# The opening of a one-core layer kernel by quarters of the channels, and a new order of its gates

## The chip, the core and the metric

One core of a Trainium2 chip. The metric is the device time of one execution in microseconds; the kernel before takes 708.6 us (median of three runs, 707.45 to 708.78). All data are f32. Products of activations with the big weights are split: a tile is cut into a high part (rounded to fp32r) and a low remainder, and a product is high x high + high x low + low x high, three fp32r matmuls.

## What is computed

One layer of a hybrid encoder, 256 tokens of 1024 channels, cut from the reference to what the change touches:

```python
c_act = jax.nn.silu(c)
mod = c_act @ ada_w[l] + ada_b[l]
sh1, sc1, gt1, sh2, sc2, gt2 = [m[:, None, :] for m in jnp.split(mod, N_MOD, axis=-1)]
h = rms_norm(x, norm1_g[l]) * (1.0 + sc1) + sh1
proj = h @ w_in[l]
q, k, v, g_out, gk_low, z, xbc, dt_raw, gates = split_cols(proj, IN_SIZES)
o_a = gla_mixer(q, k, v, g_out, gk_low, ...)
o_b = ssd_mixer(z, xbc, dt_raw, ...)
```

After it come the merge of both branches, a mixture of 32 experts (96 MB of weights) and the last norm. In the GLA mixer k is scaled by exp of sums of gates (gk), each chunk of 64 tokens gives an update k^T v, and the states follow by a recurrence over four chunks. In the SSD mixer a matrix exp(-|sum of rates|) per head is multiplied by C B^T of the chunk.

## The kernel before

**Pieces and units.** The weights come from HBM in pieces of 1 MB (128 partitions x 2048). The eight early pieces (modulation blocks 2, 0, 3, 1, two halves each: shift and scale of the first norm) have places of their own; all others go through a ring of five slots, in the order of `PIECES` (lines 70 to 77). ScalarE casts a piece to its high part (line 613, three high slots), VectorE subtracts for the low part (line 895). `before(name)` (lines 601 and 886) makes an engine do all splits that are due before the named step, one or two pieces ahead of it: this fixes where they stand in each engine's order. A unit is 512 output columns, two pieces: xbc 0 to 7 (channel-major: 96 matmuls of 256 columns), then k, q, v 0, v 1, g 0, g 1, z, gate and so on; k, v, g, z are token-major (48 matmuls of 512 columns). Units use PSUM banks 0 to 3 in turn, everything else ("mix") banks 4 to 7 in turn, by `PLAN` (lines 88 to 115). TensorE's order is written by hand (lines 1604 to 1793); all engines run in order and wait on semaphores; a bank is asked for with `begin` (line 1476), which waits until its last user has been read.

**The start.** Small parameters and x (transposed, x_t) are loaded, then the early pieces, with the first ring piece fourth. ScalarE squares x_t, TensorE sums by ones, VectorE computes 1/rms by a bit trick and three Newton steps of three operations (lines 909 to 917). Modulation blocks are matmuls with 32 columns of activations; VectorE transposes (line 903), adds the bias, scales x and writes h by channel tile (line 930), ScalarE rounds it to the high part (line 627), VectorE subtracts for the low part (line 935). Blocks 2 and 0 serve channels 0 to 511, then 3 and 1 the rest, so the first half of xbc 0's first half-unit (lines 1543 to 1550) runs once half the channels are there. Between these steps TensorE runs filler matmuls on ones, `keep_clock` (line 1489).

**The convolutions.** Each half-unit of xbc is copied from PSUM (line 653), convolved by VectorE in eight steps (lines 988 and 991), and given to Silu (line 639). After xbc 0 comes the small projection ("small", lines 1630 to 1636); VectorE reads it after the second convolved group (line 959), ScalarE takes Exp and Ln (lines 659 to 662). Modulation blocks 4 to 9 follow xbc 0 to 5.

**The middle.** TensorE runs k, q, sums over gates (gsuf, gdec), v 0, sums of rates of token tile 0 (four banks, "arow"), v 1, sums of tile 1, C B^T of both tiles ("cb"), g 0, GLA updates of tile 0 ("gU", four banks), g 1, updates of tile 1, z 0. VectorE subtracts in each arow bank (line 1036), multiplies the decay matrix by cb (line 1045), and copies or accumulates the updates (lines 1058 and 1060). ScalarE takes Abs and Exp of the decay matrix (lines 707 and 708) and Silu of g (line 713).

```python
            for i in range(2):
                project(("g", i))
                if i == 0:
                    pe.wait_ge(kdec_done, TT)
                ...
                gla_updates(i)
```

## Time and profile before

| | |
|---|---|
| median of the runs | 708.6 us |
| span of the profiled execution | 709.2 us |
| TensorE busy | 683.8 us, 96% |
| VectorE busy | 398.5 us, 56% |
| ScalarE busy | 258.5 us, 36% |
| GpSimd busy | 70.8 us, 10% |
| mean DMA | 283 GB/s; 420 GB/s from 532 to 670 us |

The profile is of one execution, whose own time is its span, 709.2 us, 0.6 over the median of the runs. Busy time of TensorE includes the filler matmuls. Two levels of TensorE's clock occur, 2.4 GHz (shown as 1.00) and 1.2 GHz (0.50). PE is TensorE, DVE VectorE, ACT ScalarE, POOL GpSimd, SPq the DMA-issuing queue of SyncE. A line can be that of a helper: 1487 is every matmul, 895 and 613 every split.

### The profile page before, as it was taken

To read this page: it belongs to the slowest core of one execution; us is meant where nothing else is said; L and a number is where in the kernel's file an instruction comes from. 1 tells how busy PE (TensorE), PEld (TensorE's weight loads), DVE (VectorE), ACT (ScalarE), POOL (GpSimd) and SP (SyncE) were. 2 spreads that over 40 slices of the span, in tenths; PEclk is the share of its full clock that TensorE was granted. 3 is DMA by queue.
4 is the path that set the end of the run, shared out by engine and by line. 5 is a ranking of instruction groups with operands and counts; after the bars stand their busy time and mean duration, and the time that the engine had idled before them with its cause. 6 is when DMAs were issued, how large, how long until landed. Compare 5 with 4: busy or idle time off the path is not lost.

```text
span 709.2 us, 13401 instructions
## 1 busy us (share of the span) xinstructions
PE 683.8 (96%) x5734; PEld 552.0 (78%) x5734; DVE 398.5 (56%) x684; ACT 258.5 (36%) x365; POOL 70.8 (10%) x69
## 2 busy tenths in 40 slices
PE   8998999999999999999999999999999999999893
PEld 8898999999878777899989998766666666665441
DVE  3567677985785687987857467454324122221226
ACT  2344454547474442435544333232131221221003
POOL 0010000000000814400000000001112111111111
PEclk9999999999999999999999999999999999999997
DMA  9989677655435433336568658989999999999982
GB/s 366 414 310 374 247 269 272 245 176 187 165 119 178 172 126 119 119 120 238 179 238 286 241 202 312 372 293 392 419 376 420 420 420 421 418 419 419 419 340 100
DMA packets 31054, 200.76 MB, mean 283 GB/s; under 512 B 5031, under 2 KB 5415, under 8 KB 7826
## 3 DMA queue, kind: packets, MB, share of 16 engines
q1 hardware_dynamic: 27378, 193.27, 70.9%
q0 software_dynamic: 3616, 6.62, 2.6%
q8 instruction: 46, 0.75, 0.4%
q14 instruction: 14, 0.11, 0.0%
HBM read 194.83 MB, written 10.75 MB: 290 GB/s over the span
## 4 chain that ended last, share of the span: by engine, by line
PE 78%; DMA 9%; SPq 5%; DVE 4%; ACT 2%; issue 2%; DVEq 0%; ACTq 0%
PE ps L1487 76%; SPq L449 4%; DMA ring<-in_expert_pieces 4%; DMA r_kq<-in_pieces 3%; DVE ring_rounded L895 2%; DMA ring<-in_pieces 2%; ACT ring_rounded L613 1%; PE ps L1599 1%; PE ps L1903 1%; SPq L446 0%; DVE r_lm L1036 0%; DVE r_kq L1107 0%; DVE r_xs_rounded L1163 0%; ACT r_lm L707 0%; DVE r_kq L1101 0%
## 5 line engine op out<-in xcount | busy, mean ns | idle before, releaser
L895 DVE TENSOR_TENSOR ring_rounded<-ring,ring_rounded 128x2048 fp32r<-128x2048 f32 x60 | 138.2, 2308 | 70.0 <-ACT ring_rounded L613 69.8
L1487 PE MATMUL ps<-hT_rounded,ring_rounded 128*128 128x256 f32 x832 | 155.1, 286 | 2.0 <-DVE ring_rounded L895 2.0
L1487 PEld LDWEIGHTS ps<-hT_rounded,ring_rounded 128*128 128x128 f32 x832 | 131.9, 193 | 4.7 <-issue 4.7
L613 ACT CAST ring_rounded<-ring 128x2048 fp32r<-128x2048 f32 x60 | 114.2, 1905 | 55.4 <-PE ps L1487 27.9
L1487 PE MATMUL ps<-x_sb_rounded,ring_rounded 128*128 128x256 f32 x416 | 118.4, 285 | 0.0
L1487 PE MATMUL ps<-ring_rounded,hT_rounded 128*128 128x512 f32 x352 | 109.5, 392 | 0.0
L1487 PEld LDWEIGHTS ps<-x_sb_rounded,ring_rounded 128*128 128x128 f32 x416 | 80.4, 193 | 0.3 <-issue 0.2
L1487 PEld LDWEIGHTS ps<-ring_rounded,hT_rounded 128*128 128x128 f32 x352 | 65.3, 188 | 14.9 <-issue 1.7
L572 POOL DMA_INDIRECT y_rows<-r_st,r_btm x29 | 28.4, 981 | 348.6 <-DVE r_st L1370 348.6
L819 ACT ACTIVATE sq<-ps 128x128 f32<-128x128 f32 x32 | 8.9, 277 | 142.5 <-PE ps L1487 142.5
L1487 PE MATMUL ps<-ring,r_lm 128*64 128x256 f32 x512 | 59.2, 380 | 1.2 <-DMA ring<-in_expert_pieces 1.2
L1370 DVE TENSOR_TENSOR r_st<-ps,r_kq 128x512 f32<-128x512 f32 x32 | 22.1, 691 | 64.9 <-PE ps L1487 64.9
L1487 PEld LDWEIGHTS ps<-ring,r_lm 128*64 128x64 f32 x512 | 36.6, 137 | 27.5 <-issue 7.9
L1487 PE MATMUL ps<-ring_rounded,x_sb_rounded 128*128 128x512 f32 x144 | 56.0, 389 | 0.0
L1346 DVE TENSOR_SCALAR r_btm<-ps,par 128x1 int32<-128x1 f32 x29 | 6.2, 219 | 74.0 <-PE ps L1903 74.0
L1487 PE MATMUL ps<-r_lm_rounded,ring_rounded 128*128 128x256 f32 x256 | 46.2, 283 | 0.0
L810 ACT ACTIVATE r_lm<-ps,mod 128x256 f32<-128x256 f32 x60 | 30.5, 560 | 42.1 <-PE ps L1487 42.1
L1487 PEld LDWEIGHTS ps<-r_lm_rounded,ring_rounded 128*128 128x128 f32 x256 | 40.0, 192 | 0.0
L991 DVE SCALAR_TENSOR_TENSOR r_lm<-r_lm,par 128x255 f32<-128x255 f32 (+2 forms) x96 | 39.1, 476 | 0.0
L1487 PE MATMUL ps<-r_xs_rounded,ring_rounded 128*128 128x256 f32 x128 | 36.2, 283 | 0.0
L562 POOL TENSOR_TENSOR r_v<-r_xs,dtb 128x512 f32<-128x512 f32 x8 | 13.3, 1666 | 221.2 <-PE ps L1487 212.2
L1487 PE MATMUL ps<-r_pv_rounded,r_ct_rounded 128*128 128x256 f32 x128 | 33.8, 301 | 0.0
(324 smaller groups left out, 1019.3 us busy)
## 6 DMA issues: line engine op xcount, KB each, us to landing
ring<-in_pieces SPq DMA_DIRECT2D x74, 1024.0 KB, 5.0
ring<-in_expert_pieces SPq DMA_DIRECT2D x48, 1024.0 KB, 18.9
r_z<-in_expert_pieces SPq DMA_DIRECT2D x12, 1024.0 KB, 12.6
r_xs<-in_expert_pieces SPq DMA_DIRECT2D x12, 1024.0 KB, 14.2
g_sb<-in_expert_pieces SPq DMA_DIRECT2D x6, 1024.0 KB, 13.0
r_st<-in_expert_pieces SPq DMA_DIRECT2D x6, 1024.0 KB, 14.4
r_bt<-in_expert_pieces SPq DMA_DIRECT2D x6, 1024.0 KB, 18.4
hT<-in_expert_pieces SPq DMA_DIRECT2D x6, 1024.0 KB, 17.6
```

The lines of the kernel that those rows point to most:

```text
L449: sp.dma_start(moe_slots[MOE_SLOT[j]], expert_pieces[j]).then_inc(moe_full[MOE_SLOT[j]], 16)
L562: link(nc.gpsimd.tensor_tensor(heads(xdt[:, b, t]), heads(src[:, t]), over(dt[:, t, h], SP_), ALU.mult))
L572: pool.indirect_dma_start(out=y_rows[:, :], out_offset=bass.IndirectOffsetOnAxis(ap=idx_i[:, e:e + 1], axis=0), in_=y_row[:, e % 2], in_of ...
L613: nc.scalar.copy(high_of(p_), slot_of(p_)).then_inc(hi_ok, 1)
L810: ins = nc.scalar.activation(hsel[:, m // 4 % 2, k].rearrange("p e r -> p (e r)"), ps[m if m < 4 else 4 + m % 4][:, a * 4 * W:(a + 1) * 4 ...
L819: nc.scalar.activation(hid_s[:, e % 2], ps[e % 2][:, 0:P], ACT.Silu).then_inc(silu_up, 1)
L895: nc.vector.tensor_tensor(low_of(p_), slot_of(p_), high_of(p_).bitcast(F32), ALU.subtract).then_inc(lo_ok, 1)
L991: ins = nc.vector.scalar_tensor_tensor(acc[:, a, tap:], u[:, a, 0:T - tap], w, acc[:, a, tap:], ALU.mult, ALU.add)
L1370: nc.vector.tensor_tensor(y_row[:, e % 2], ps[2 + e % 2][:], gt2_two, ALU.mult).then_inc(y_out, 1)
L1487: return nc.tensor.matmul(o, l, r, start=start, stop=stop)
L1599: ins = nc.tensor.transpose(bank[:, at:at + P], src, ident)
L1903: nc.tensor.transpose(ps[e % 2][:, 2 * P:3 * P], hid[:, e % 2], ident).then_inc(turned, 1)
```

## The change

The early pieces are now four quarters of the channels, each with both shift and scale for two channel tiles ("quarter" q). The units xbc 0, k and q are computed together, in six banks, as pieces land: a "pair" piece holds two channel tiles of xbc 0 and k, a "rest" piece four channel tiles of q. After quarter q's modulation its two tiles of h are made, ScalarE writing the high part directly from x, and the products of pair q and of the rest follow. x_t is issued first. The squares are made by VectorE, and 1/rms by Sqrt on ScalarE, a reciprocal and one Newton step. Filler is run before the sum of squares and once after quarter 0 only. Modulation blocks 4 to 9 follow xbc 1 to 6. In the middle the order becomes v 0, v 1, arow of tile 0, gsuf, gdec, g 0, arow of tile 1, g 1, cb, gU of both tiles, z 0, and ScalarE's and VectorE's orders follow it. k and q are copied from PSUM beside the first convolutions. The diff, cut:

```diff
-ADA_AFTER = {("xbc", i): 4 + i for i in range(6)}
-ADA_FIRST = [2, 0, 3, 1]
-ADA_ORDER = ADA_FIRST + list(range(4, 10))
+ADA_AFTER = {("xbc", i): 3 + i for i in range(1, 7)}
+QUARTERS = KD // 2
+ADA_ORDER = [("quarter", q) for q in range(QUARTERS)] + [("ada", i) for i in range(4, 10)]
+START = [("pair", 0, 0, 0), ("rest", 0, 0, 0), ("pair", 1, 0, 0), ("pair", 2, 0, 0), ("rest", 1, 0, 0), ("pair", 3, 0, 0)]
+FIRST_UNITS = [("xbc", 0), ("k", 0), ("q", 0)]
...
+PLAN = ["sumsq"] + ADA_ORDER[:QUARTERS]
+PLAN += [("unit", "xbc", 0), ("unit", "k", 0)] + [("q", h) for h in range(2)] + ["small"]
+for _i in range(1, 8):
+    PLAN += [("unit", "xbc", _i)]
...
+PLAN += [("unit", "v", 0), ("unit", "v", 1)] + [("arow", 0, j) for j in range(4)]
+PLAN += [("gsuf", 0), ("gsuf", 1), "gdec", ("unit", "g", 0)] + [("arow", 1, j) for j in range(4)]
+PLAN += [("unit", "g", 1), ("cb", 0), ("cb", 1)] + [("gU", c, hp) for c in range(NC) for hp in range(2)]
...
+MIX_BANK = {n: 4 + (i - len(MIX)) % 4 for i, n in enumerate(MIX)}
+MIX_BANK.update({("q", 0): 4, ("q", 1): 5})
+MIX_BANK.update({n: 6 + i % 2 for i, n in enumerate(["sumsq"] + ADA_ORDER[:QUARTERS])})
+MIX_TURN = {n: [MIX_BANK[m] for m in MIX[:i]].count(MIX_BANK[n]) for i, n in enumerate(MIX)}
...
+            sp.dma_start(xT, x_t).then_inc(s_xT, 16)
...
+            for n, p_ in enumerate(START):
+                if p_[0] == "pair":
+                    for h in range(2):
+                        p_q = ("quarter", p_[1], h, 0)
+                        sp.dma_start(slot_of(p_q), piece_src(p_q)).then_inc(early_full[EARLY.index(p_q)], 16)
+                load_piece(n, p_)
+            sp.dma_start(wsm, small_w).then_inc(s_small, 16)
+            sp.dma_start(wgk2, gk2_rows).then_inc(s_small, 16)
+            sp.dma_start(par[:, NCOL:], params[:, NCOL:]).then_inc(s_const, 16)
...
+            mix_taken(act, "sumsq")
+            nc.scalar.activation(norm_s, norm_m, ACT.Sqrt).then_inc(x_sqrt, 1)
+            for q in range(QUARTERS):
+                act.wait_ge(mod_ok, q + 1)
+                for k in (2 * q, 2 * q + 1):
+                    nc.scalar.activation(h_parts[0][:, k], xT[:, k], ACT.Identity, scale=mod[:, 8 + k:9 + k],
+                                         bias=mod[:, k:k + 1]).then_inc(h_hi, 1)
+                split_to(START.index(("pair", q, 0, 0)) + 1 + (q in (0, 2)))
...
+                    if g == 1:
+                        for t in range(TT):
+                            bank = unit_wait(act, ("k", 0), t)
+                            nc.scalar.copy(k_tm[:, t], bank[:]).then_inc(unit_used(("k", 0), t), 1)
+                        for h in range(2):
+                            bank = mix_wait(act, ("q", h))
+                            nc.scalar.mul(qT[:, 2 * h:2 * h + 2].rearrange("p h t -> p (h t)"), bank[:], HK ** -0.5).then_inc(
+                                mix_used(("q", h)), 1)
...
+            values(0)
...
+            values(1)
...
+            decay_matrix(0)
+            output_gate(0)
+            decay_matrix(1)
+            output_gate(1)
...
+            for q in range(QUARTERS):
+                ks = slice(2 * q, 2 * q + 2)
+                nc.vector.tensor_tensor(x_sqT[:, ks], xT[:, ks], xT[:, ks], ALU.mult).then_inc(x_sq, 1)
...
+            dve.wait_ge(x_sqrt, 1)
+            link(nc.vector.reciprocal(norm_y, norm_s))
+            link(nc.vector.tensor_tensor(norm_s, norm_y, norm_y, ALU.mult))
+            link(nc.vector.scalar_tensor_tensor(norm_s, norm_s, -0.5, norm_m, ALU.mult, ALU.mult))
+            link(nc.vector.scalar_tensor_tensor(norm_y, norm_s, 1.5, norm_y, ALU.add, ALU.mult))
...
+            def quarter(q):
+
+                bank = mix_wait(dve, ("quarter", q))
+                turned_ = ada_turned[:, q % 2]
+                nc.vector.transpose(turned_.rearrange("p m c -> p (m c)"), bank[:, 0:P]).then_inc(mix_used(("quarter", q)), 1)
+                mix_taken(dve, ("quarter", q))
+                two = lambda ap: ap.rearrange("p (a k) -> p a k", a=2)[:, :, 2 * q:2 * q + 2]
+                link(nc.vector.tensor_tensor(two(mod[:, 0:16]), turned_[:, :, 0].rearrange("p (a k) -> p a k", a=2),
+                                             two(col("ada_b", 0, 16)), ALU.add))
+                scale = mod[:, 8 + 2 * q:10 + 2 * q]
+                nc.vector.scalar_tensor_tensor(scale, scale, 1.0, col("norm1", 2 * q, 2), ALU.add, ALU.mult).then_inc(mod_ok, 1)
+                dve.wait_ge(mod_ok, q + 1)
+                for k in (2 * q, 2 * q + 1):
                     nc.vector.tensor_scalar(h_f[:, k], xT[:, k], mod[:, 8 + k:9 + k], mod[:, k:k + 1], ALU.mult,
                                             ALU.add).then_inc(h_full, 1)
-                for i in (2 * n_, 2 * n_ + 1):
-                    dve.wait_ge(h_hi, i + 1)
-                    ks = slice(2 * i, 2 * i + 2)
-                    nc.vector.tensor_tensor(h_parts[1][:, ks], h_f[:, ks], h_parts[0][:, ks].bitcast(F32), ALU.subtract
-                                            ).then_inc(h_lo, 1)
+                dve.wait_ge(h_full, 2 * q + 2)
+                dve.wait_ge(h_hi, 2 * q + 2)
+                ks = slice(2 * q, 2 * q + 2)
+                nc.vector.tensor_tensor(h_parts[1][:, ks], h_f[:, ks], h_parts[0][:, ks].bitcast(F32), ALU.subtract
+                                        ).then_inc(h_lo, 1)
...
+            normalised(0)
+            for q in range(QUARTERS):
+                quarter(q)
+                if q + 1 < QUARTERS:
+                    normalised(q + 1)
+                split_to(START.index(("pair", q, 0, 0)) + 1 + (q in (0, 2)))
...
+            spread_rates(0)
+            dve.wait_ge(gk_l, 1)
+            nc.vector.scalar_tensor_tensor(gk_ls, gk_ls, 0.0, gk_abs, ALU.min, ALU.subtract).then_inc(gk_done, 1)
+            before((("v", 1), 1))
+            dve.wait_ge(silu_done, 16)
+            for t in range(TT):
+                mix_taken(dve, ("tr", 5, t))
+            differences(0)
+            for t in range(TT):
+                before(("gsuf", t))
+                mix_taken(dve, ("gsuf", t))
+                unit_taken(dve, ("k", 0), t)
+                nc.vector.tensor_tensor(k_tm[:, t], k_tm[:, t], gsuf_e, ALU.mult).then_inc(kdec_done, 1)
+            spread_rates(1)
+            for t in range(TT):
+                before((("g", 0), t))
+            differences(1)
...
+            def products_of_start(p_, q):
+
+                w = [v.rearrange("p a b -> p (a b)").rearrange("p (u k n) -> p u k n", u=2, k=2) for v in (high_of(p_), low_of(p_))]
+                units_ = ("xbc", "k") if p_[0] == "pair" else ("q",)
+                for n_, (a_, b_) in enumerate(((0, 0), (0, 1), (1, 0))):
+                    if n_ == 0:
+                        pe.wait_ge(hi_ok, SPLIT_AT[p_] + 1)
+                        pe.wait_ge(h_hi, 2 * q + 2)
+                    elif n_ == 1:
+                        pe.wait_ge(h_lo, q + 1)
+                    else:
+                        pe.wait_ge(lo_ok, SPLIT_AT[p_] + 1)
+                    for kk in range(2):
+                        k = 2 * q + kk
+                        first, last = k == 0 and n_ == 0, k == KD - 1 and n_ == 2
+                        for i, u in enumerate(units_):
+                            w_k = w[a_][:, i if p_[0] == "pair" else q % 2, kk]
+                            h_k = h_parts[b_][:, k]
+                            if u == "k":
+                                for t in range(TT):
+                                    bank, b, _ = unit(("k", 0), t)
+                                    ins = mm(bank[:], h_k[:, t * P:(t + 1) * P], w_k, first, last)
+                                    if last:
+                                        ins.then_inc(bank_full[b], 1)
+                                continue
+                            for a in range(4):
+                                bank, b = unit(("xbc", 0), a // 2)[:2] if u == "xbc" else mix(("q", a // 2))[:2]
+                                ins = mm(bank[:, a % 2 * T:(a % 2 + 1) * T], w_k[:, a * P:(a + 1) * P], h_k,
+                                         first and a % 2 == 0, last and a % 2 == 1)
+                                if last and a % 2:
+                                    ins.then_inc(bank_full[b], 1)
+                return ins
...
+            modulation(("quarter", 0))
+            keep_clock(12)
+            products_of_start(("pair", 0, 0, 0), 0).then_inc(start_read, 1)
+            modulation(("quarter", 1))
+            products_of_start(("rest", 0, 0, 0), 0)
+            products_of_start(("rest", 0, 0, 0), 1).then_inc(start_read, 1)
+            products_of_start(("pair", 1, 0, 0), 1).then_inc(start_read, 1)
+            modulation(("quarter", 2))
+            products_of_start(("pair", 2, 0, 0), 2).then_inc(start_read, 1)
+            modulation(("quarter", 3))
+            products_of_start(("rest", 1, 0, 0), 2)
+            products_of_start(("rest", 1, 0, 0), 3)
+            products_of_start(("pair", 3, 0, 0), 3)
...
+            project(("v", 0))
+            project(("v", 1))
+            rows_of_sums(0)
             pe.wait_ge(gk_done, 1)
...
+            project(("g", 0))
             rows_of_sums(1)
+            project(("g", 1))
...
+            pe.wait_ge(kdec_done, TT)
+            for name in (("v", 0), ("v", 1)):
+                for t in range(TT):
+                    unit_taken(pe, name, t)
+            for t in range(TT):
+                gla_updates(t)
```

## Rows read from the trace of the kernel before

**Rows 1.** The chain that ended last, whole span: start us, us, engine line, instructions

```profile
5.69 23.92 DMA r_kq<-in_pieces
...
35.51 14.31 PE ps L1487 x168
49.83 11.98 DMA ring<-in_pieces
...
66.21 13.24 PE ps L1487 x96
...
199.71 4.34 DVE ring_rounded L895 x2
...
644.78 27.52 DMA ring<-in_expert_pieces
```

**Rows 2.** Timeline of TensorE: start us, us, instruction, idle before and its releaser

```profile
7.30 3.72 PE L1487 MATMUL ps<-r_lm,ones 128*128 128x256 f32 x16 [1.03 <-ACT r_lm L621]
...
32.20 3.29 PE L1487 MATMUL ps<-ones 128*128 128x128 f32 x28
...
44.22 3.67 PE L1487 MATMUL ps<-r_z 128*128 128x48 f32 x32
...
205.04 2.08 PE L1487 MATMUL ps<-r_ct,r_bt 128*64 128x64 f32 x64 [1.07 <-DVE r_lm L1036]
```

**Rows 3.** Busy time by stretch: TensorE, weight loads, VectorE, ScalarE, GpSimd, clock, DMA

```profile
64.20:66.21 2.01, 0.03 (x4) 0.03 (x1) 2.01 (x2) 2.01 (x5) 0.00 (x0) 1.00 1.07 379
66.44:69.85 3.41, 3.41 (x18) 3.41 (x18) 3.41 (x8) 1.07 (x1) 0.00 (x0) 0.50 0.93 363
80.00:203.90 123.90, 123.90 (x1061) 113.73 (x1059) 95.46 (x136) 68.05 (x73) 0.00 (x0) 1.00 0.63 222
218.16:220.09 1.93, 1.93 (x17) 1.46 (x17) 1.93 (x1) 1.82 (x2) 0.00 (x0) 1.00 0.50 76
```

**Rows 4.** Groups of VectorE, whole span: shapes, count, busy us, mean ns, idle before

```profile
L895 DVE TENSOR_TENSOR ring_rounded<-ring,ring_rounded 128x2048 fp32r<-128x2048 f32 x60 | 138.2, 2308 | 70.0 <-ACT ring_rounded L613 69.8
...
L1036 DVE TENSOR_TENSOR r_lm<-ps,dtb 128x512 f32<-128x512 f32 x8 | 5.0, 681 | 0.0
L1060 DVE SCALAR_TENSOR_TENSOR r_st<-r_st,gdec,ps 128x256 f32<-128x256 f32 x12 | 4.9, 474 | 0.0
...
L1045 DVE TENSOR_TENSOR r_lm<-r_lm,ps 128x2048 f32<-128x2048 f32 x2 | 4.6, 2282 | 1.9 <-ACT r_lm L708 1.9
```

**Rows 5.** Timeline of VectorE, start of the kernel

```profile
11.06 0.42 DVE L909 TENSOR_SCALAR r_lm<-ps 128x256 f32<-128x256 f32 x1 [9.96 <-PE ps L1487]
...
30.87 0.32 DVE L903 STREAM_TRANSPOSE r_st<-ps 128x128 f32<-128x128 f32 x1 [3.54 <-PE ps L1487]
...
31.61 1.38 DVE L930 TENSOR_SCALAR r_z<-r_xs,mod 128x256 f32<-128x256 f32 x4
...
39.99 2.45 DVE L991 SCALAR_TENSOR_TENSOR r_lm<-r_lm,par 128x255 f32<-128x255 f32 x6
```

**Rows 6.** Timeline of ScalarE around two table loads

```profile
49.43 0.26 ACT L661 ACTIVATE dt_abs<-dt_abs 128x64 f32<-128x64 f32 x1 [2.35 <-DVE dt_abs L948]
...
173.17 1.28 ACT L688 ACT_TABLE_LOAD   x1
175.95 0.60 ACT L688 ACTIVATE r_pv<-ps 128x512 f32<-128x512 f32 x1 [1.50 <-PE ps L1487]
```

**Rows 7.** DMA issues: KB each, us from issue to landing (issued at 2.10 and 5.21)

```profile
g_sb<-in_pieces SPq DMA_DIRECT2D x1, 1024.0 KB, 9.0
...
r_xs<-in_pieces SPq DMA_DIRECT2D x1, 1024.0 KB, 21.9
```

**Rows 8.** Groups of ScalarE, whole span

```profile
L613 ACT CAST ring_rounded<-ring 128x2048 fp32r<-128x2048 f32 x60 | 114.2, 1905 | 55.4 <-PE ps L1487 27.9 <-DMA ring<-in_pieces 27.5
L810 ACT ACTIVATE r_lm<-ps,mod 128x256 f32<-128x256 f32 x60 | 30.5, 560 | 42.1 <-PE ps L1487 42.1
...
L707 ACT ACTIVATE r_lm<-r_lm 128x2048 f32<-128x2048 f32 x2 | 3.8, 1919 | 7.9 <-DVE r_lm L1036 7.9
```

267 lines of the change are left out of this document (84 added, 183 removed).

## The prediction

> **What bounds it now.** I read the chain of waits first [rows 1]. After 35.5 us it is almost all TensorE. It starts in a transfer: the eighth piece of modulation weights lands at 5.69 + 23.92 = 29.6 us, and until 35.51 TensorE has mostly run filler products. It leaves TensorE again at 49.83 (a ring piece lands at 61.84) and at 199.71 (two low-half subtractions of VectorE, each of which must precede the next step by the order of the code). At 644.78 expert weights take over; the loads there are released by TensorE's progress, so I take a shift of the work before them over one to one, in both directions.
>
> How much of TensorE's time is not work? A projection product of 256 columns takes 0.121 us: 168 products from 35.51 to 49.83 are 72 of these, the small projection of 3.6 and two halves of modulation of 1.9 together [rows 1, 2]. So a unit (96) takes 11.6 us, and the same in token-major form (48 of 512 columns). Up to 66.21 the work is 3.7 (sum of squares) + 8 early halves at 1.0 + two units 23.2 + 3.6 + two modulations 3.8 + transposes 1.0 = 43.3. So 22.9 us are filler or idle, and the third unit takes 13.24 instead of 11.6, because after 2.0 us of idle, with modulation products before it, the granted clock is 0.50 for 3.4 us [rows 3]: 24.5 lost. This is what the change is after. From 80 us on TensorE is never idle [rows 3] until 203.97, where it waits 1.07 us for VectorE to free the first cb's bank [rows 2].
>
> **The new start.** Times are from the start of the span, at full clock. x_t is issued first, so it lands about 0.5 us earlier; VectorE squares it by quarters (0.7 each, as a 128x512 operation [rows 4]; an f32 product of two SBUF tiles). TensorE begins the sum of squares at 6.4 instead of 7.30 and ends at 10.05. A step of the 1/rms chain is 0.42 + 0.04 us [rows 5]: mean, Sqrt on ScalarE, reciprocal and three steps are 2.9 us instead of twelve steps; normalising two channel tiles takes 0.7. That is done at 13.7. No row shows a reciprocal of 256 columns: not under the 0.42 of a simple step, not over four of them; I take 0.42, the nearest rows, and the end moves by at most 1.3 us. The Sqrt needs its own table, and Silu needs a reload after it. Table loads here start before the wait that precedes their function: 173.17 + 1.28 = 174.45, and idle counts from there to 175.95 [rows 6]. So the Sqrt load is hidden by the sum of squares, the Silu load by the first convolution.
>
> Pieces land 2.5 us apart: 5.21 + 21.9 = 27.1 for the seventh early one, 29.6 for the eighth [rows 7, 1]; the second, which is where quarter 0's second half will be, at 2.10 + 9.0 = 11.1. The new order puts quarter 0 at 11.1, pair 0 near 14, quarter 1 at 22.1, quarter 2 at 29.6, quarter 3 at 39.6. After the last product of a quarter's modulation comes a fixed chain: transpose, bias and scale 0.95 (30.87 to 31.61 and 0.2 to start [rows 5]), two Identity passes of ScalarE 0.9 (0.56 from PSUM for one [rows 8], less from SBUF), then, by ScalarE's order, the pair's high half 1.9 [rows 8]: 3.75 us. A pair is 5.8 us of products, two tiles of q 2.9.
>
> Quarter 0 is modulated at 12.1; its chain waits for 13.7, so pair 0 can start at 17.2: after 2.8 us of filler (24 records; 28 take 3.3 [rows 2]) 2.3 us idle. Pair 0 to 23.0, modulation 1 to 25.0, q of quarters 0 and 1 to 30.8 (this covers chain 1), pair 1 to 36.6, modulation 2 to 38.6. Nothing covers chain 2, although pair 2 has long landed: **idle 3.75**. Pair 2 to 48.15, modulation 3 to 50.15, q to 55.95, pair 3 to 61.75, small to 65.35, first half of xbc 1 to 71.15. Its second piece is late: VectorE convolves two groups after xbc 0 is full (61.3), 3.1 us each (six of the eight steps take 2.45 [rows 5]), only then reads small; ScalarE does Exp, table load, Ln (0.26 + 1.28 + 0.26, by the load and the Exp in [rows 6]) before it casts that piece, and the low half ends at 74.5: **idle 3.35**. Today a modulation of 1.9 us stands between small and this unit and small comes earlier beside the convolutions. xbc 1 ends 80.3, transposes and one modulation 83.2.
>
> Work by then: 3.7 + 8.0 + 34.8 + 3.6 + 11.6 + 1.0 + 1.9 = 64.6, lost 18.6. The start gains 24.5 - 18.6 = **5.9 us at full clock**. But three idle stretches of 2.3, 3.75 and 3.35 us stand where one of 2.0 cost 1.6 us, and most of the filler is gone. Between none and three falls (0 to 4.8 us) I take two, 3.2: the longest lies behind modulation products, as today's did. **Start: -2.7 us.**
>
> **The reordered middle.** k and q have left, so v 0 follows xbc 7. The chain of the gates (one 128x1024 Exp, Ln, five smaller steps, VectorE's minimum) is hidden by v 0 and v 1, 22 us long. The k and q copies move to ScalarE's stretch beside small, 2.3 us, before VectorE needs it. Count from the end of v 1. The sums of rates of tile 0 take 1.8, then gsuf 0 needs the bank of the first of them; VectorE gets to its subtraction only after the low half of g's second piece, whose cast stands behind v 1's first copy: free at 2.7, **idle 0.9**. g 0 then runs to 17.3, sums of tile 1 to 19.1, g 1 to 30.2. Then cb 0, cb 1 (2.0 us [rows 2]) and gU of tile 0 come **without a projection between them**. The bank rotation gives gU(1,0) and gU(1,1) the banks of cb 0 and cb 1, and all four banks are asked for before the first product. So TensorE waits for VectorE's two multiplications by cb, 2.28 us each [rows 4]; today g 0 hides them. They are late themselves: the order demands z 0's two low halves first. ScalarE: decay matrix of tile 1 (Abs and Exp, 1.92 each [rows 8]) from 21.8 to 25.6, z 0's first cast to 27.5, Silu's table to 28.8, one g copy to 29.4, second cast to 31.3. VectorE: low half to 33.6, cb 0 to 35.9, cb 1 to 38.2. TensorE was ready at 32.2: **idle 6.1**. gU of tile 0 (1.93 [rows 3]) ends at 40.2; gU of tile 1 asks for its four banks at once, which come free when VectorE has taken eight blocks (0.47 or less each [rows 4]), at 42.6: **idle 2.4**; today g 1 hides this. Sum 9.4, less today's 1.1: 8.3. An idle 6.1 is three times the one after which the clock fell; I charge 1.6 and 1.0 more because gU then runs at 0.50 in the chain. **Middle: +10.9 us** (8.3 at full clock, 12 if the second gap prolongs the fall).
>
> A rule of the Trainium skill speaks against this part (ScalarE: Activation LUTs, "Table sets: the hidden batching unit"): group activations by table set. The change alternates Exp, Silu, Exp, Silu, two loads more than today; the page prices a switch at 1283 ns plus a drain of about 1380. The trace agrees on the load and not on the drain: idle counts from the load's end. With the drain the second cast would come 1.4 us later and the forecast would be 1.4 higher.
>
> **At no cost:** SyncE's order and the constants behind the start (needed first at 80); the zeroing of rows, now at 61 us beside one piece with 10 us of slack (if not, 2 us); the renumbered banks, whose turns are the same; the tail.
>
> **Sum.** -2.7 + 10.9 = +8.2 on the profiled span of 709.2, which stands 0.6 above the median 708.6 of the runs: 708.6 + 8.0 = **716.6 us**. Differences under 0.2% (1.4 us) can't be told from none.
>
> **Rivals.** *The clock hardly falls* (17%): idle is broken by short bursts. For it: the gaps of 1.03 and 1.07 us that cost no clock [rows 2]. Against: the fall after 2.0. Then -5.9 + 8.3 = +2.4: 711.0. *The banks do not bind* (16%, the faster side): the wait at cb is the one term that decides the sign. If the two multiplications are over when gU asks, because ScalarE casts z 0 earlier or VectorE has slack I don't see, the middle is 0.9 - 1.1 and the start alone counts: 702.5 (full clock) to 705.7. It decides where the two gaps together fall below the start's gain of 2.7 to 5.9 us; for it: VectorE is busy just 56% of the span; against: every one of its steps above is forced by the code's order, as the 1.1 us at 203.9 shows today. *The start is not reached* (7%): quarters land late or VectorE and ScalarE run behind in chains 1 and 3 too; 3 to 5 us more, 720 to 722. The forecast itself, 712 to 720.5, has 60%. A result within 0.2% comes only where terms cancel.
>
> Range 706.0 to 721.0: below lie most of the bank rival's chance, above half of the last. Faster 0.16, same 0.06, slower 0.78.
>
> **What would show it.** Right: no filler after 15 us; gaps near 38.6 and 71 to 74; TensorE's clock at 0.50 once or twice before 80 us; xbc 2 starting with k and q done at 83 to 87; after g 1 an idle stretch of TensorE released by the cb multiplication (L1045 today), 4 us or more, and one by the gU copies. Wrong: gU directly behind cb, or xbc 2 before 80 us.

## The result

The changed kernel takes 727.3 us (median of 4 runs, 726.38 to 727.88), the kernel before 708.65 (4 runs, 707.45 to 708.78): ratio 1.0263, 95% interval 1.0248 to 1.0277. It is slower, as forecast, but by 18.7 us, not 8, and outside the range.

The page of the kernel after, its span and busy parts, two rows of the 40 slices, and the shares of its chain:

```profile
span 726.1 us, 13249 instructions
PE 682.2 (94%) x5650; PEld 548.8 (76%) x5650; DVE 399.6 (55%) x685; ACT 263.8 (36%) x371; POOL 70.7 (10%) x69
PE   7879899999998699999999999999999999999893
PEclk9999999999999599999999999999999999999998
PE 79%; DVE 7%; DMA 5%; ACT 4%; issue 3%; SPq 2%; DVEq 0%; POOL 0%; ACTq 0%; POOLq 0%
```

TensorE and VectorE are busy for as long as before to within 2 us (683.8 and 398.5 us then, filler included); ScalarE is busy 5.3 us longer, 5.1 of it four more table loads. So the loss is waiting and clock, not work. The 14th slice stands out: TensorE about 60% busy, at half clock. The chain of waits up to there, where the chain of before leaves TensorE three times in the first 205 us (start us, us, what; "issue" is a table load or the engine's own overhead; steps left out are marked):

```profile
0.98 9.40 PE ps L1526 x44
...
10.91 1.28 ACT L630
...
12.73 1.76 DVE r_lm L928
...
15.90 0.70 DVE r_xs L936
...
17.37 1.09 ACT hT_rounded L634 x2
18.46 1.80 ACT ring_rounded L623
20.30 22.63 PE ps L1526 x248
...
44.21 0.59 ACT hT_rounded L634
44.80 1.80 ACT ring_rounded L623
46.63 20.16 PE ps L1526 x180
...
75.90 1.80 ACT ring_rounded L623
77.72 2.30 DVE ring_rounded L907
80.16 7.47 PE ps L1526 x48
...
161.06 2.29 DVE ring_rounded L907
163.35 0.61 DVE g_sb L1004
164.01 0.66 PE ps L1645 x4
...
202.32 0.69 DVE r_lm L1057
203.15 11.92 PE ps L1526 x56
...
222.32 1.92 ACT r_lm L694
224.29 1.26 issue
225.55 1.92 ACT r_lm L695
...
227.81 1.47 issue
229.28 1.25 ACT L701
230.57 0.60 ACT g_sb L701
231.17 1.80 ACT ring_rounded L623
233.13 2.07 issue
235.20 4.49 DVE r_lm L1084 x2
239.82 3.76 PE ps L1526 x15
...
246.07 14.15 PE ps L1526 x56
```

The chain leaves TensorE seven times: behind modulation 0 (idle 5.14 us before 20.30), behind modulation 2 (3.75 before 46.63), inside xbc 1 (3.36 before 80.16), at the sixth transposes (0.67), before gsuf (0.98), before gU of tile 0 (7.34) and of tile 1 (2.46). The last three take the place of the one wait of 1.07 us at 203.97 [rows 2]; the first three, of the idle 2.0 us and the filler in [rows 2, 3].

TensorE's clock, in windows of the kernel after (stretch, length, busy and count of PE, PEld, DVE, ACT, POOL, then the granted clock):

```profile
20.15:23.50 3.35, 3.20 (x12) 2.93 (x13) 3.15 (x2) 1.90 (x2) 0.00 (x0) 0.51 1.01 418
47.45:50.85 3.40, 3.40 (x13) 2.98 (x13) 3.40 (x2) 0.94 (x1) 0.00 (x0) 0.52 0.07 31
81.60:84.95 3.35, 3.35 (x18) 3.35 (x18) 3.35 (x5) 0.31 (x1) 0.00 (x0) 0.52 0.02 7
235.20:252.20 17.00, 9.91 (x38) 7.45 (x39) 10.77 (x19) 0.04 (x1) 1.91 (x2) 0.50 0.00 0
90.31:178.10 87.79, 87.12 (x954) 83.86 (x951) 65.18 (x119) 40.56 (x45) 0.00 (x0) 1.00 0.77 283
```

So three falls of the size of the one in [rows 3] in the start, and one of 17 us in the middle, in which TensorE worked for 9.9 us at 1.2 GHz.

**Where the 16.9 us between the two spans lie.** Up to the start of xbc 2, by the sums of the prediction, 64.6 us of work end at 90.31: 25.7 lost against 24.5, +1.2; and 0.8 more, because k in token-major form took 10.9 us in the trace of before and not the 11.6 that I had counted (start together +2.0). Convolutions: +1.2, of which 0.67 is the wait at 164.01. From the end of the convolutions to the end of z 0, without k and q: 83.9 us against 69.4, +14.5. From there to the end: 464.1 us against 464.9, -0.8. Sum 16.9.

The medians differ by 1.8 more. Every run of which time and span are both shown has a time 1.8 to 2.5 us above its span (727.88 and 726.1 for this profile). So the span of 709.2 was not that execution's own time, as was said ahead of the prediction: it probably took about 711.0, 2.3 above its median and not 0.6, while the profile after took 0.6 more than its median. That difference of 1.8 lies in no stage of the two traces. The mean granted clock of that profile was 0.992, and in other executions of the same kernel it went up to 0.996, which is also the mean of a later version (c1 below) whose trace has no fall before its last 6 us; so the fall in [rows 3] probably does not come in every execution.

### The profile page after: what moved, and what is told of

It reads as the page before. It is cut to its first block, busy times and chain, and to the rows that moved or that the text cites. A ratio compares the mean times of both kernels' runs of the same rounds, so it can differ in the third digit from the quotient of the medians.

```text
span 726.1 us, 13249 instructions
## 1 busy us (share of the span) xinstructions
PE 682.2 (94%) x5650; PEld 548.8 (76%) x5650; DVE 399.6 (55%) x685; ACT 263.8 (36%) x371; POOL 70.7 (10%) x69
## 4 chain that ended last, share of the span: by engine, by line
PE 79%; DVE 7%; DMA 5%; ACT 4%; issue 3%; SPq 2%; DVEq 0%; POOL 0%; ACTq 0%; POOLq 0%
PE ps L1526 77%; DMA ring<-in_expert_pieces 4%; ACT ring_rounded L623 2%; SPq L454 2%; DVE ring_rounded L907 2%; DMA ring<-in_pieces 1%; PE ps L1645 1%; PE ps L1942 1%; DVE r_lm L1084 1%; DVE r_lm L1020 1%; DVE r_lm L1057 0%; DVE r_kq L1146 0%; DVE r_xs_rounded L1202 0%; ACT r_lm L695 0%; ACT r_lm L694 0%
## 5 line engine op out<-in xcount | busy, mean ns | idle before, releaser
L1526 PE MATMUL ps<-hT_rounded,ring_rounded 128*128 128x256 f32 x832 | 151.6, 289 | 12.2 <-ACT ring_rounded L623 8.9
L1526 PE MATMUL ps<-ring_rounded,hT_rounded 128*128 128x512 f32 x352 | 111.8, 399 | 0.0
L1526 PE MATMUL ps<-x_sb_rounded,ring_rounded 128*128 128x256 f32 x416 | 110.3, 286 | 0.0
L1526 PEld LDWEIGHTS ps<-x_sb_rounded,ring_rounded 128*128 128x128 f32 x416 | 77.6, 194 | 1.1 <-issue 0.2
L1526 PE MATMUL ps<-ring,r_pv 128*64 128x512 f32 x128 | 31.0, 604 | 1.9 <-issue 1.8
```

Source lines behind the costliest of these rows:

```text
L1526: return nc.tensor.matmul(o, l, r, start=start, stop=stop)
```

## The experiments

My theory has three parts: the middle is VectorE's and ScalarE's forced order in front of two banks; each gap of the start is order too, a serial chain with no work beside it; and the clock charges gaps beyond their length. Against each stands a rival: a transfer or another engine is late there, or the clock is only a symptom. Each run is the changed kernel with one edit unless its heading says more; ratios are to the kernel before, run beside it. Where a gain is given against 727.3, it compares runs of different groups; the kernel before, run beside each group, had medians of 707.6 to 709.1, so such a difference is good to about 1 us.

**One table is needed to read the runs.** The clock did not fall alike in them, even where the code was the same, so an edit's worth is read in its own stage. The table has, from the trace of each run, how long the clock was at 0.50 in the first 100 us and in the middle, when gsuf starts, and how long it is from there to gO, the products that follow z 0 (and gU of tile 1 where that was moved):

| run | start: us at 0.50 | gsuf starts | middle: us at 0.50 | gsuf to gO |
|---|---|---|---|---|
| changed kernel | 10.2 | 203.15 | 17.1 | 58.82 |
| m1, cb before g 1 | 13.6 | 202.80 | 3.4 | 50.14 |
| m2, gU apart too | 13.6 | 204.01 | 0 | 46.59 |
| m3, filler in the middle | 10.2 | 203.44 | 0 | 54.25 |
| m4, cb before a low half | 13.6 | 203.29 | 10.2 | 54.23 |
| m5, Exp's table ahead | 10.2 | 203.56 | 10.2 | 56.19 |
| s1, chain of before | 10.2 | 202.67 | 17.1 | 58.77 |
| s2, Sqrt's table ahead | 10.2 | 201.78 | 10.2 | 57.61 |
| s5, one wait | 13.6 | 202.42 | 10.2 | 57.58 |
| s3, cast ahead | 10.2 | 199.81 | 17.1 | 58.72 |
| s4, split before small | 6.8 | 198.64 | 10.2 | 57.55 |
| s6, filler too long | 3.4 | 206.14 | 10.2 | 57.59 |
| s8, filler of right length | 3.4 | 201.10 | 10.2 | 57.42 |

The eight rows with the unedited middle (the changed kernel and s1 to s8) show two levels, 58.7 to 58.8 us and 57.4 to 57.6: about 1.2 us of the differences between their times is this alone. And gsuf starts at 202.8 to 204.0 in the six with the unedited start.

### Both multiplications by cb before g 1

```diff
-PLAN += [("unit", "g", 1), ("cb", 0), ("cb", 1)] + [("gU", ...
+PLAN += [("cb", 0), ("cb", 1), ("unit", "g", 1)] + [("gU", ...
             rows_of_sums(1)
-            project(("g", 1))
             for t in range(TT):
                 bank = begin(("cb", t))
...
+            project(("g", 1))
```

> Edit: the products cb of both token tiles run before g 1 instead of after it; all else as in the changed kernel (profiled 726.1 us, median 727.3). Theory A (bank wait): the 7.3 us that TensorE stands before the first gU are the wait for VectorE's two multiplications by cb, which the order puts behind two low halves. With g 1 between cb and gU the wait before the first gU is gone; cb itself waits 1 to 3 us for VectorE's differences; the 2.5 us between the two gU stay; the 17 us at 0.50 clock shrink to 3.4 or none. Span 717 to 719.5. Rival B (transfers or ScalarE's cast of z's second piece hold TensorE): the idle stretch moves but keeps its length, span above 723.

Measured 718.03 us, ratio 1.0135 [1.0104, 1.0167], 9 us faster than the change as it stands. No wait before gU of tile 0; 0.97 before cb, 3.14 before gU of tile 1, and in the middle one clock fall of 3.4 us. A projection beside the two multiplications is worth 9 us, 8.7 by the table's last column. The wait between the two gU did not stay at 2.5, as expected, but grew.

### The same, and gU of tile 1 behind z 0

```diff
-            for t in range(TT):
-                gla_updates(t)
+            gla_updates(0)
...
                         mix_taken(pe, ("q", h))
+                    gla_updates(1)
```

(with the banks planned in that order)

> Edit: as m1, and gU of token tile 1 runs after z 0, so that z 0 stands between the two gU. Theory A: the 2.5 us before the second gU go too, and with them the rest of the slow clock; in exchange gO may wait about 1 us for VectorE's eight accumulations. Span 714 to 717.5, 2 to 4 below m1. Rival: VectorE's accumulations before gO cost as much as the gap gave: within 1 us of m1.

Measured 716.77 us, 1.0127 [1.0097, 1.0157]: 1.3 us below the run before, less than the 2 to 4 expected, because its gsuf starts 1.2 us later, before any edited step; the stage itself is 3.6 us shorter (table). TensorE in the middle of this version, one window over all of it:

```profile
205.00:260.00 55.00, 53.08 (x324) 42.64 (x323) 36.67 (x40) 32.81 (x39) 9.72 (x10) 1.00 0.35 118
```

Full clock throughout, 1.9 us idle. From gsuf to gO 12.2 of the 14.5 us that the middle had lost are back: that much is the order of these pieces of work. What is left are waits of 0.97 us each before gsuf and cb and of 0.94 before gO.

### Filler in the two gaps of the middle

```diff
+            unit_taken(pe, ("g", 0), 1)
+            keep_clock(30)
             gla_updates(0)
+            keep_clock(9)
             gla_updates(1)
```

> Edit: 30 filler matmul calls (6.9 us at full clock) between cb and the first gU and 9 (2.1 us) between the two gU; no wait is taken away. Theory: the clock's part of the middle is 5 us (gU twice 1.9 and z's first products), apart from the idle time. Then the clock stays at 1.00 there and the span is 720.5 to 722.5. Rival: the waits alone set the end and the slow clock cost nothing beside them: 725.5 to 727.

Measured 723.25 us, 1.0218 [1.0195, 1.024]. Nothing useful comes earlier by the order of the code, and yet the span falls by 4.8 us. One window over both gaps in each version, filler first:

```profile
239.00:252.00 13.00, 12.29 (x81) 10.36 (x80) 9.64 (x18) 0.00 (x0) 4.92 (x3) 1.00 0.01 1
```

```profile
239.00:252.00 13.00, 9.71 (x37) 7.34 (x38) 6.76 (x17) 0.00 (x0) 1.71 (x2) 0.50 0.00 0
```

That is the price of the clock in the middle: 4.6 us by the table, 4.7 from the trace of the changed kernel (gU 3.79 and 3.72 us instead of 1.93 and 1.92, z 0 12.18 instead of 11.15). It is the price in an execution with 17.1 us at 0.50. In the five with the same gaps and 10.2 us at 0.50 it is 3.2 to 3.4 us, and the medians of this run and the changed kernel differ by about 4.

### The multiplications before z 0's low halves on VectorE

```diff
-                before(("cb", t))
+                split_to(29)
```

> Edit: VectorE makes only the first of z's two low halves before the multiplications by cb, the second after them. Theory A: multiplications start when cb is full (about 231.5 instead of 235.2), so the first gap falls from 7.3 to about 4; the second low half now stands before the gU copies, so the second gap grows from 2.5 to about 3.5 to 4.5. Span 722 to 725. Rival (the multiplications are not what is waited for): gaps unchanged, 726.

Measured 723.23 us, 1.02 [1.0171, 1.0229]. The first wait falls from 7.34 to 3.74 us; the second stays (2.43) and does not grow, as was expected. So one forced low half, with the wait for its cast, is half of the first wait, as the prediction's chain had it.

### Exp's table ahead of the Abs of tile 1

```diff
             def decay_matrix(t):
+                if t:
+                    nc.scalar.activation(dt_abs[:, 0, 0:1], dt_abs[:, 0, 0:1], ACT.Exp)
```

> The changed kernel with one 1-element-wide Exp on ScalarE before the Abs of tile 1, so that Exp's table is loaded in ScalarE's idle 3.9 us before that Abs, and not between Abs and Exp. Theory A (the idle time before gU is VectorE's and ScalarE's forced chain, and the load I left out is all of the difference to 6.1 us): the idle stretch falls from 7.34 to 6.05 us and the time by 1.3 us, to 725.5 to 726.5. Theory B (another step is late, the cb products or a landing): it falls by less than 0.5 us.

Measured 726.2 us, 1.0242 [1.0214, 1.027]. The first gU product of this version and its wait (start us, us, what, idle and releaser):

```profile
238.98 3.62 PE L1528 MATMUL ps<-r_v,r_kq 64*128 64x256 f32 x16 [6.06 <-DVE r_lm L1086]
```

6.06 is the forecast's 6.1. The 7.34 was that chain and one table load of 1.28 us that I had not counted: g 0's Silu had taken Exp's place. Against the five runs with the same 10.2 us at 0.50, this one is 1.2 to 1.4 us shorter from gsuf to gO, again the load.

### The 1/rms chain of before

```diff
-            dve.wait_ge(x_sqrt, 1)
-            link(nc.vector.reciprocal(norm_y, norm_s))
-            ... (three steps)
+            (two integer steps, three Newton steps of three)
```

> The changed kernel with the 1/rms chain of before (two integer steps and three Newton steps on VectorE, no Sqrt, no reciprocal). Removed: a table load of 1.28 us that begins only after the mean is done, Sqrt 0.3, reciprocal 1.75 and the three steps after it. Added: eleven steps at about 0.46 us, 5.1 us. Theory A (the square root's gain is eaten by its table load behind the wait and by a reciprocal four times as long as a simple step): the two chains are equally long within 0.5 us, pair 0 starts at 20.0 to 20.6 us against 20.30, and the time is that of the changed kernel, 726.5 to 728 us. Theory B (the square root did shorten the chain, as the prediction had it): pair 0 starts 2 us or more later and the time is 729 to 731 us.

Measured 727.24 us, 1.0258 [1.0241, 1.0275]; from the start of the sum of squares to pair 0 it takes 13.39 us (6.45 to 19.84) instead of 13.55 (6.75 to 20.30). The square root, meant to save six steps, saves nothing. Why is in two rows of VectorE in the changed kernel (start us, us, what, idle before):

```profile
12.73 1.75 DVE L928 RECIPROCAL r_lm<-r_lm 128x256 f32<-128x256 f32 x1 [1.90 <-ACT r_lm L630]
14.52 0.42 DVE L929 TENSOR_TENSOR r_lm<-r_lm 128x256 f32<-128x256 f32 x1
```

The 1.90 is the wait for ScalarE: table load 1.28 and Sqrt 0.42. The reciprocal takes 1.75 us, 4.2 times a product of the same shape.

### A Sqrt of one column ahead of the wait

```diff
+            link(nc.scalar.activation(gss[:, 0, 0, 0:1], ones[:, 0:1], ACT.Sqrt))
             mix_taken(act, "sumsq")
             nc.scalar.activation(norm_s, norm_m, ACT.Sqrt)
```

> The changed kernel with one 1-element-wide Sqrt on ScalarE ahead of the wait for the sum of squares, so that Sqrt's table is there when the mean is. Theory A (the load lies in the chain): the load of 1.28 us leaves the chain, pair 0 starts at 19.0 us instead of 20.30, and the time falls by 1.3 us to 725.5 to 726.5 us, more only if the clock fall after it goes too. Theory B (pair 0 waits for something else, a weight piece or ScalarE's other work): pair 0 stays at 20.3 us and the time is that of the changed kernel, 727.3 us.

Measured 725.22 us, 1.0219 [1.0193, 1.0244]: 2.1 us less than 727.3. From the start of the sum of squares to pair 0 it is 12.26 us instead of 13.55: the load was in the chain. gsuf starts 1.4 us earlier, which is the edit; the rest of the 2.1 is the shorter fall of the clock in the middle.

### One wait instead of two before the Sqrt

```diff
-            link(nc.scalar.activation(col("c", 0, 8), col("c", 0, 8), ACT.Silu))
+            n[0] += 1
+            nc.scalar.activation(col("c", 0, 8), col("c", 0, 8), ACT.Silu).then_inc(s_act, 1)
             mix_taken(act, "sumsq")
             nc.scalar.activation(norm_s, norm_m, ACT.Sqrt).then_inc(x_sqrt, 1)
+            act.wait_ge(s_act, 1)
```

> The changed kernel with nothing added and nothing left out: only ScalarE's wait for its own second Silu is moved from before the Sqrt to behind it. In the changed kernel two waits stand before the Sqrt, and in the compiled order of instructions the first of them sits on the table load, the second on the Sqrt; with one wait the load carries none. Theory A (the load waits because it carries the sum's wait): the load now starts right after the second Silu at about 7 us, pair 0 starts 1.28 us earlier against the end of the sum of squares, and the time is 725 to 726.3 us. Theory B (the load always follows the last wait before its function, and the one at 173 us of the kernel before was something else): the load stays at 10.9 us, the time at 727.3.

Measured 725.82 us, 1.0239 [1.021, 1.0267]; from the start of the sum of squares to pair 0 12.37 us instead of 13.55. In the compiled order of ScalarE's instructions (a line of its own for a wait that is an instruction of its own), changed kernel first:

```
wait bank_free6
ACT_TABLE_LOAD
ACTIVATE L630 [waits s_act_chain]

ACT_TABLE_LOAD
ACTIVATE L631 [waits bank_free6]
```

And in the traces of the two, in the same order:

```profile
10.91 1.28 ACT L630 ACT_TABLE_LOAD   x1 [4.07 <-DVE r_lm L924]
12.21 0.42 ACT L630 ACTIVATE r_lm<-r_lm 128x256 f32<-128x256 f32 x1
```

```profile
6.83 1.28 ACT L631 ACT_TABLE_LOAD   x1
10.68 0.42 ACT L631 ACTIVATE r_lm<-r_lm 128x256 f32<-128x256 f32 x1 [2.56 <-DVE r_lm L926]
```

The load stands behind one of the waits where two stand before the function, and behind none where there is one. [rows 6] showed the second kind (a wait for PE alone); I took it for a rule.

### Casting a pair ahead of its quarter's chain

```diff
             for q in range(QUARTERS):
+                if q:
+                    split_to(START.index(("pair", q, 0, 0)) + 1)
                 act.wait_ge(mod_ok, q + 1)
```

> The changed kernel with each pair from the second on cast to its high half by ScalarE before it waits for the modulation of that quarter, instead of behind the chain. Theory A (the fixed chain of 3.75 us behind modulation 2 is half cast): the idle stretch before pair 2 falls from 3.75 to about 1.9 us, the time by 1.9 us, and by 1.6 us more if the clock no longer falls behind it: 724 to 725.5 us. Theory B (pair 2 waits for its weights or for VectorE's low half): the idle stretch stays over 3 us and the time within 0.6 us of 727.3.

Measured 725.49 us, 1.024 [1.0222, 1.0257], in the profile 3.2 us less. The wait before pair 2 is 2.05 us, and the clock stayed at 1.00 behind it: xbc 1's late products start 3.36 us earlier (76.80), 1.8 by pair 2's earlier start and 1.6 by the fall that did not come. The clock fell twice later, at 67 to 71 us, straight behind the small projection, and at 77 to 82. The wait in xbc 1 is 1.88 us instead of 3.36, but that is no second gain: m1, whose start was not edited, shows the same 1.88 and the same fall behind the small projection (70 to 75). What VectorE finishes late, TensorE waits for less if it arrives more slowly.

### xbc 1's second piece split before small

```diff
-                    before("small")
+                    split_to(8)
```

(on ScalarE and on VectorE)

> The changed kernel with xbc 1's second piece cast and its low half taken before ScalarE's Exp, table load and Ln and before VectorE reads the small projection. Theory A (TensorE's idle 3.36 us at about 77 us is this order alone): the stretch falls to under 0.5 us and the clock fall behind it (3.4 us at 0.50, worth 1.6 us) goes with it: 3 to 5 us less, 722 to 724.5 us. Theory B (the piece itself is late, or the convolutions of xbc 0 hold VectorE): the stretch stays above 2 us and the time above 725.5 us.

Measured 721.76 us, 1.0183 [1.0166, 1.02]: 5.5 us less, of which 4.5 are there when gsuf starts and about 1.2 are the shorter fall of the clock in the middle. From 70 to 90 us, where the changed kernel is 16.64 us busy at 0.91:

```profile
70.00:90.00 20.00, 20.00 (x217) 19.63 (x217) 17.30 (x35) 15.27 (x18) 0.25 (x1) 1.00 0.89 316
```

### Filler in two gaps of the start, too long and of the right length

```diff
-            keep_clock(12)
+            keep_clock(12 + 40)
             products_of_start(("pair", 0, 0, 0), 0)
...
             modulation(("quarter", 2))
+            mix_taken(pe, ("quarter", 1))
+            keep_clock(28, mix(("quarter", 1))[0])
```

> The changed kernel with 40 more filler products (0.118 us each) behind modulation 0 and 28 behind modulation 2, in the two long gaps of the start. No work is earlier or later by the order of the code. Theory A (each of these gaps costs its idle time and then 1.6 to 1.7 us for a clock fall behind it): the granted clock stays at 1.00 from 15 to 60 us and the time falls by 3.2 us to 723.5 to 724.7. Theory B (filler is no work to the clock's control, or a fall comes anyway from the modulation products): the clock still falls and the time is 727.3 or, where the filler ends after the gap would have, more.

Measured 728.76 us, 1.0295 [1.0249, 1.0341]: a miss of my own making. A call of the filler's loop leaves two product records, not one; the filler ran 3.7 and 2.5 us past its gaps. The next run has 20 and 14.

> The changed kernel with 40 more filler records (4.4 us at 0.11 us) behind modulation 0, whose gap is 5.14 us, and 28 (3.1 us) behind modulation 2, whose gap is 3.75 us. The earlier run with filler had 80 and 56 records: the clock stayed at 1.00 from 0 to 60 us, but the filler ended 3.6 and 2.5 us after the gaps would have. Theory A (each gap costs a clock fall of 1.6 to 1.7 us besides its idle time): clock 1.00 from 15 to 60 us, work in place, 3.2 us less: 723.5 to 724.7 us. Theory B (filler costs as much as it saves): 726.5 to 728 us.

Measured 724.28 us, 1.0216 [1.0187, 1.0244]. Its window over both gaps:

```profile
12.00:60.00 48.00, 47.58 (x530) 43.94 (x523) 28.46 (x39) 17.48 (x17) 0.00 (x0) 1.00 0.83 334
```

No fall, and xbc 1's late products start 3.05 us earlier (77.11 instead of 80.16): each of the two falls had cost 1.5 us. The medians differ by 3.0 and the spans by 3.4, but that is not the two falls alone: 1.0 us is lost again at the sixth transposes, which wait 1.24 us for VectorE here, and 1.4 comes from gsuf to gO, where the clock was low for 10.2 us and not 17.1.

### All repairs together, with and without more filler

The edits above (one wait, casts ahead, for pair 0 too, xbc 1's split, cb before g 1, gU apart), the first with 14 calls of filler in each start gap.

> The changed kernel with all repairs together: both multiplications by cb before g 1, gU of the two tiles apart, one wait before the Sqrt, each pair cast ahead of its chain (pair 0 too), xbc 1's second piece split before small, and 14 filler products in each of the two start gaps. If each gap is a term of its own: 727.3 - 10.5 (middle) - 1.3 (load) - 1.9 (cast before chain 0) - 1.9 (before chain 2) - 5.5 (split) - 3.2 (two clock falls) = 703.0, range 701.5 to 705. If the gaps only move on (a later wait for VectorE or a landing takes over): 706 to 712, not under the kernel before.

> All repairs of the run before without the added filler. The two start gaps are then about 2 us each. If each costs a clock fall: 3.2 us above the version with filler, about 706. If gaps of 2 us cost no clock here: within 0.5 us of it.

Measured 705.89 us, 0.9955 [0.994, 0.997], and 706.19 us, 0.9966 [0.9944, 0.9988]: both faster than the kernel before, by 0.5% and 0.3%, little but clear of the intervals. The filler, counted in calls once more, ran past its gaps: pair 2 starts 1.9 us later than without it. Without it the start gaps were 1.74 and 2.05 us, and in the profiled execution the clock did not fall in them, but once at 63 us, straight behind the small projection, with no gap near. That is one execution of ten: their times go from 703.7 to 708.9 us, with mean clocks of 0.996 down to 0.991, and the three fastest (703.7 to 704.2) have 0.995 or 0.996; with the filler nine executions lie within 705.2 to 707.3, eight of them at 0.995 or 0.996. So the equal medians are no proof that gaps of 2 us cost no clock. In other executions it was low for longer, and where is not on record. The sum of single gains, 703.0, was 2.9 us too low, 1.9 of it this filler in the first of the two; part of the rest is that the single gains had the shorter fall of the middle in them.

### The same with VectorE's low halves behind the small waits

```diff
-                        before(("gklin", t))
                         bank = mix_wait(dve, ("gklin", t))
...
+                    before((("xbc", g // 2), g % 2))
```

(only for g == 12; and the same in the differences of the gates' sums; filler 6 and 7 calls)

> All repairs (as in c1) with short filler in the two start gaps (12 records, 1.3 us, and 14, 1.5 us, against idle 1.74 and 2.05 us without any), and VectorE's low halves behind the four differences of the gates' sums and behind the gklin copies instead of before them. If the waits 0.67, 0.98 and 0.97 us are that order alone they go: about 2.5 us under c1 and c2 (705.9 and 706.2), 0.9 us more because c1's filler ran 1.3 and 1.0 us past its gaps: 702.0 to 704.0. If the low halves are then late for g 0 and g 1, new waits of up to 2.3 us stand before these and the time is 705 to 708.

Measured 703.26 us, 0.9924 [0.9907, 0.9942] (the trace is of its slowest execution, 706.61). The wait at the sixth transposes is gone; those before gsuf and cb stayed at 0.98 and 0.97, because earlier lines of the code had already called for the same low halves, so that half of the edit moved nothing. The last run moves them in fact:

```diff
-            before((("v", 1), 1))
+            split_to(min(PIECES_OF[("v", 1), 1] + AHEAD_OF[("v", 1), 1], len(SPLITS)) - 1)
...
+            before((("g", 0), 0))
             differences(1)
+            before((("g", 0), 1))
```

> The repaired version of the run before, with one low half of VectorE (2.29 us) moved behind the four differences of the gates' sums at both tiles. Theory A (the waits of TensorE of 0.98 us before gsuf and 0.97 us before cb are this low half in front of the first difference): both waits fall under 0.2 us, and the time is 1.9 us less than 703.3: 700.8 to 702.2. Theory B (the differences wait for the last sums, or the low halves are late for g 0 and g 1 in their new place): waits of 0.5 us or more stay, or new ones appear, and the time is 702.5 to 704.

Measured 701.46 us, 0.9916 [0.9897, 0.9935], the best version found: 25.8 us below the change as it stands, 6.1 below the kernel before (707.59 beside it). VectorE and TensorE at the first of the two places:

```profile
183.52 2.28 DVE L910 TENSOR_TENSOR ring_rounded<-ring,ring_rounded 128x2048 fp32r<-128x2048 f32 x1
186.88 2.48 DVE L1060 TENSOR_TENSOR r_lm<-ps,dtb 128x512 f32<-128x512 f32 x4 [1.08 <-PE ps L1530]
187.95 1.88 PE L1530 MATMUL ps<-g_sb,par 128*128 128x512 f32 x4
189.29 2.28 DVE L910 TENSOR_TENSOR ring_rounded<-ring,ring_rounded 128x2048 fp32r<-128x2048 f32 x1
```

Now VectorE waits for TensorE, and gsuf starts without idle time. Both waits are gone; the low halves are not late in their new place.

## Why the forecast was right in direction and wrong in size

**The mechanism and the sign held.** The prediction's deciding term was the bank wait at cb and gU, and that is where the change loses: 14.5 of 16.9 us. With a projection put between cb and gU and one between the two gU, the same kernel takes 716.8, and with the start's order mended too it beats the kernel before. By the spans the forecast missed 8.7 us: 4.7 in the start, 3.6 in the middle, 1.2 in the convolutions, and 0.8 the other way behind z 0. Step by step:

- **Idle before gsuf 0.9:** 0.98. Its cause (the low half of g's piece before the difference) is shown by the last run.
- **Idle before gU 6.1 and between its tiles 2.4:** 7.34 and 2.46. *Failed by one table load.* The working has Abs and Exp of tile 1 "from 21.8 to 25.6", with no load between them, although g 0's Silu runs before. The run with the load hidden gives 6.06. The prediction's own sentence on the page of the skill counts this load (Exp, Silu, Exp, Silu: two more than before); its working has only Silu's.
- **Clock in the middle 2.6:** 4.7. *Mis-sized term.* I took one fall of the length in [rows 3]; the clock stayed at 0.50 for 17 us over two gaps and gU between them, and in five other runs with the same gaps for 10.2 us, at 3.2 to 3.4 us. The prediction had this as "12 if the second gap prolongs the fall", for the whole middle, which is 3.7 for the clock and covers those five; with the load, that bound would have been 13.3.
- **Pair 0 at 17.2, idle 2.3:** 20.30 and 5.14. *Two steps failed.* "So the Sqrt load is hidden": no, because of its two waits; 1.28 us. "I take 0.42" for the reciprocal: 1.75, inside the bound I had given (1.3 more), but at its far end. The sum was against twelve steps of 0.46, and the run with these twelve steps (s1) is as fast. Of the rest, 0.25 is the sum of squares' later end (10.3) and 0.2 the two Identity passes (1.09 against 0.9).
- **Idle 3.75 behind modulation 2 and 3.35 inside xbc 1:** 3.75 and 3.36. These held to 0.01 us. The second is shown to be order alone by its removal; the first was cut to 2.05 by the order of ScalarE's cast, and the rest is the chain of transpose, bias and Identity.
- **Clock in the start, two falls, 3.2:** three, 4.8 at 1.6 each. *Mis-sized term.* The bound was named ("between none and three"); I chose low. Other runs with the same start were at 0.50 for 13.6 us and not 10.2, so even three falls are not the most it can be. Start in all: +2.0 instead of -2.7.
- **At no cost, the renumbered banks and their turns:** *failed by 0.7.* The sixth transposes need the bank of the gates' first copy, which VectorE makes behind a low half of a late piece (151.27 and 159.13 in the trace's chain, 161.06 and 163.35 above). 0.5 us of the convolutions' 1.2 is not placed.
- **"708.6 + 8.0":** the 8.2 was worked out from the trace of an execution that stands about 2.3 above its median, not 0.6. 1.8 us of the miss are this, as told above, and in no stage.

Of the rivals, the one that the banks don't bind is refuted by the first two runs. "The clock hardly falls" is refuted by the windows. "The start is not reached" has the right size, 4.7 us, by luck: its condition (quarters late, or VectorE and ScalarE behind in chains 1 and 3 too) did not come about, as there is no gap behind modulations 1 and 3. The 4.7 are chain 0 (the Sqrt's load, which I had argued away, and the reciprocal) and the third fall. It had 7% and was not combined with the upper end of the middle. That is the mistake in the range: reciprocal (1.3), third fall (1.6) and the longer fall in the middle (1.1) had named upper bounds, all on the same side, 4.0 together, and 721.0 is 4.4 above the forecast: nothing was left for a load or two in the wrong place (1.3 each) and for the span taken as a time (1.8).

The rule of the Trainium skill that spoke against this part (ScalarE: Activation LUTs, "Table sets: the hidden batching unit": group activations by table set) was the better guide than my working: ScalarE's compiled order has 17 table loads against 13 before, and three of the four new ones (Sqrt, Exp, Silu) lie in the chain that sets the end, 3.8 us, of which I had counted one. The drain that the same page of the Trainium skill adds to a switch (section "What ACT_TABLE_LOAD costs") is not in the trace: the load at 224.26 ends at 225.54 and Exp starts at 225.55. The row that the prediction took for this, [rows 6], could not tell, since its 1.50 us of idle time would have hidden a drain of 1.38.

## What to carry to other kernels

Count the work that stands between a product and the next use of its bank, not only how much work there is: the change moved a projection of 11 us from between cb and gU, and the same VectorE steps that nobody had waited for became 10 us of idle time. Before putting a function on ScalarE into a chain, write down which table is active and how many waits stand before it, and try its load ahead. And a kernel that has lost its filler can pay for a gap twice, so mend the longest gaps first, and try filler (counted in the trace, not in the code) before judging what remains. Read an edit's worth in the stage that it touches: here the clock moved the time of whole runs by 1 to 3 us in stages that the edit had left alone.

## What the runs showed of the hardware

- A table load of 1.28 us stood ahead of a function with one wait and started early (6.83), but behind the first of two waits (10.91).
- VectorE's reciprocal of 128x256 f32 took 1.75 us, a product, a mean or a step of the same shape 0.42.
- The same idle stretches did not cost the same clock each time. After 7.34 and 2.46 us TensorE ran at 0.50 for 17 us in the changed kernel, and in the runs with one edit of the start for 17 us in two and for about 10 us, in two parts, in five (the third row below, 34 us at a mean of 0.85). In the start, gaps of 4.7 to 5.1, 3.75 and 3.36 us were followed by 3.4, 3.4 and 3.4 us at 0.50 in the changed kernel, and by 6.8, 6.8 and none in m2 and m4. Gaps of 1.74 and 2.05 us cost nothing in the profiled execution of the repaired version, a gap of 2.0 us before had [rows 3]. And in four runs (m1, s3, c2, c3) the clock fell for 3.4 us straight behind the small projection, with no gap. What decides this is open. The rows: the repaired version without filler, over its start gaps and over the small projection, and the kernel with filler in the start, over the two gaps of the middle:

```profile
12.00:60.00 48.00, 44.14 (x474) 40.03 (x465) 28.84 (x40) 18.30 (x17) 0.08 (x1) 1.00 0.89 352
60.00:70.00 10.00, 10.00 (x75) 10.00 (x75) 8.58 (x20) 8.62 (x12) 2.23 (x4) 0.83 0.92 301
```

```profile
228.00:262.00 34.00, 24.18 (x179) 19.08 (x177) 19.68 (x22) 10.30 (x17) 14.29 (x10) 0.85 0.25 84
```

- Filler products held the clock at 1.00 through gaps of 7.3, 5.1 and 3.75 us (m3 and s8).
